# Normalising ahead of the gate, and dense jobs in nine slots, in a two-block transformer kernel on one core

## Chip, cores and metric

The kernel runs on one core of one Trainium2 chip. The metric is device time in microseconds (us); runs of one kernel are compared by their median.

## What is computed

The reference takes x of 512 tokens by 1024 through two blocks, all in fp32. What matters here is the attention of each layer and the dense projections around it.

```python
# first block: one layer, heads of 64, 8 pairs of (head, head) in the selected branch
o_a = nsa_attention(q_a, k_cmp, v_cmp, kv[2], kv[3], kv[4], kv[5], gates_a)
merged = gate_a * (o_a @ w_up_nsa) + gate_b * (o_b @ w_up_gla)
x = x + merged @ w_out
x = x + (silu(h @ w_ffn_gate) * (h @ w_ffn_up)) @ w_ffn_down
# second block: mla, swa, fox, mla; 16 heads each
s = einsum('bqhd,bkhd->bhqk', q_blk, k) * scale      # fox adds c_q - c_k, swa a slope and a window
p = softmax(where(k_pos <= q_pos, s, NEG_INF))
o = einsum('bhqk,bkhd->bqhd', p, v)
y = (o * silu(gate)) @ w_out                         # gate = x @ (its columns of w_in)
x = layernorm(ALPHA * x + y)
```

## The kernel before, in words

x, its transpose and all tiles of a layer live in SBUF. Every dense product is made of three fp32r matmuls (`mm3`, lines 385 to 388): a weight and an activation are each split in a high and a low part. A weight piece (up to 128 x 1024) is loaded by SyncE into one of three raw slots (`Wr`), cast by ScalarE to its high part (`Wh`, line 957), and its low part is made by GpSimd (`Wl`, line 1962, called a POOL piece in the prediction); five slots hold the results. ScalarE casts a piece when it comes to a wait: `weights` (949) casts all that are due by then, three pieces ahead of TensorE (`AHEAD`).

Attention goes by pairs of heads, p = 0 to 7. A pair takes these steps:
- score (517, or 880 in swa): TensorE makes the scores in PSUM; VectorE takes the maxima (1451); ScalarE makes the exps with their sums (1015; 1319 in swa).
- norm (`normalise`, 1458; in swa lines 1873 to 1879): VectorE inverts the sums and multiplies the probabilities P, eight instructions of 128 to 512 columns (line 1468); in swa four for each of two heads, called units (1879).
- turn (542): TensorE transposes P, 20 transposes (14 in swa), and ScalarE (1034, 1327) and VectorE (1438) copy them to PT.
- value (552, or 901 in swa): TensorE multiplies with V into a bank of its own. V in the prediction's formulas is the time at which these matmuls end.
- gate (`gate_values`, 1489, line 1492): VectorE multiplies that bank with the gate of the pair, GT. GT is made by the job g_p: 24 matmuls on TensorE, a tanh on ScalarE (1039), a product on VectorE (1487).
- out (`gated`, 1041 and 1494): the result is split in high and low (1013, 1435) for the output product w_out.
- prep (mla alone): two small products of this pair's queries and keys, 15 matmuls.

Jobs are dense products that fill TensorE while a pair's softmax goes through the other engines: g_p, q_p, k_p, v (in fox one job of 24 matmuls each, v of 96), `tail` and m0 to m7 in nsa. The order of all steps is written out before the program by `pair_steps` (101), once for each stage, and every engine walks the same list in order, doing its own part of each step. A turn waits for its pair's probabilities. PSUM has eight banks, which TensorE takes in a ring; a step waits until the reader of its bank is done. `before` runs what a step needs first (`need` pulls jobs from the front of the list, in its order, until the needed one has run), `fill` runs jobs up to a quota. There are five such stages: nsa (in the first block), mla0, swa, fox, mla1. What stands between the values of a pair and the turn of the next is the time in which exps and norm of the next pair are covered; it is called an interval below.

In fox the jobs are q0, k0, v0 (before the pairs) and then g0, q1, k1, g1, q2, k2, g2, q3, k3, v1, g3, q4, k4, g4, q5, k5, g5, q6, k6, g6, q7, k7, g7.

Of the kernel before, what the change touches and what calls it, by code (L numbers as in the profile page):

```python
# [97 lines left out]
                self.seen[sem.name] = value  # L98


def pair_steps(n, jobs, started, score, value, after=lambda p: [], gates=False, spread=7):

    left, steps, waiting = list(jobs[started:]), [], []
    total = len(left)

    def run():
        steps.append(("job", left.pop(0)))

    def before(these):
        for kind, x in these:
            if kind != "need":
                steps.append((kind, x))
            while kind == "need" and x in left:
                run()

    def fill(p):
        while left and (total - len(left)) * (spread + 1) < total * (p + 2):
            run()  # L120

    before(score(0))
    steps.append(("score", 0))
    steps.append(("norm", 0))
    before(after(0))
    fill(-1)
    for p in range(n):
        steps.append(("turn", p))
        if p + 1 < n:
            before(score(p + 1))  # L130
            steps.append(("score", p + 1))
        before(value(p))
        steps.append(("value", p))
        if gates:
            before([("need", f"g{p}")])
            steps.append(("gate", p))
            waiting.append(p)
        if p + 1 < n:
            steps.append(("norm", p + 1))
            before(after(p + 1))  # L140
        fill(p)
        for _ in range(8 if p == n - 1 else 2):
            if waiting and not left:
                steps.append(("out", waiting.pop(0)))
    return steps


def program(nc, A, out):
    top = ExitStack()
    with top:  # L150
# [139 lines left out]
        for dp in range(2):  # L290
# [12 lines left out]
            if dp == 0:  # L303
                gla_steps.append(("turned", dp))
        nsa_steps = pair_steps(8, ["tail"] + [f"m{f}" for f in range(8)], 0, lambda p: [], lambda p: [])
        mla_steps = pair_steps(
            8, ["g0", "g1", "g2", "v0", "g3", "v1", "g4", "g5", "g6", "g7"], 5,
            lambda p: [("prep", 0)] if p == 0 else [], lambda p: [("need", f"v{p // 4}")],
            lambda p: [("prep", p + 1)] if p < 7 else [], gates=True)
        swa_jobs = ["k0", "q0", "q1", "q2", "v", "q3", "g0", "g1", "k1", "q4", "g2", "q5", "g3", "q6", "g4", "q7", "g5", "g6", "g7"]  # L310
        swa_steps = pair_steps(8, swa_jobs, 4, lambda p: [("need", f"k{p // 4}"), ("need", f"q{p}")],
                               lambda p: [("need", "v")], gates=True)
        fox_jobs = ["q0", "k0", "v0", "g0"]
# [1738 lines left out]
```

## Time and profile before

| | us |
|---|---|
| median of 3 runs | 2010.88 (2010.56 to 2013.05) |
| profiled execution, its own time | 2010.83 |
| its span | 2009.0 |
| TensorE busy | 1870.5 (93%) |
| VectorE busy | 996.7 (50%) |
| ScalarE busy | 727.3 (36%) |
| GpSimd busy | 622.2 (31%) |
| mean granted TensorE clock, share of full speed | 0.966 |

The pairs of nsa lie between about 240 and 373 us of the span, those of mla0 between 975 and 1117, of swa between 1196 and 1353, of fox between 1450 and 1669, of mla1 between 1811 and 1952. The time around the span, 1.8 us, is start and end of the execution. Busy time of TensorE includes time at the lower clock.

### The profile page before, as it was taken

The page shows a single profiled execution, that of the slowest core. Times are in us where ns is not written, and L with a number is a line of the kernel's source. Part 1 is how long each engine was busy: PE and PEld are TensorE (multiplying, and loading weights), DVE is VectorE, ACT ScalarE, POOL GpSimd, SP SyncE. Part 2 cuts the span into 40 slices and gives each one's busy share as a digit, 9 for nine tenths or more (in the row PEclk, how much of TensorE's full clock was granted, in tenths as well). Part 3 has the DMA queues.
Part 4 walks back from the last instruction along what each step waited for, and adds up shares of the span by engine and source line. Part 5 has one row for each costly group of instructions (what it writes and reads, how often), then busy time and mean ns, then how long its engine had stood idle before and what let it go on. Part 6 is the DMA issues. An engine that isn't in the chain of part 4 may idle for free.

```text
span 2009.0 us, 24953 instructions
## 1 busy us (share of the span) xinstructions
PE 1870.5 (93%) x10060; PEld 1478.4 (74%) x10060; DVE 996.7 (50%) x1994; ACT 727.3 (36%) x1547; POOL 622.2 (31%) x296
## 2 busy tenths in 40 slices
PE   6998799999999999998999999989999999989997
PEld 5776666788888888877666787767777777866665
DVE  4457677322311101144767456675654444466675
ACT  4332354323322222253444234442342333334450
POOL 3331111244444453423212223223323223322221
PEclk9998799999999999999999999989999999999999
DMA  5321110243333332332212222112323222311111
GB/s 160 92 76 51 45 32 25 71 132 109 95 101 99 95 105 84 104 90 48 45 41 77 63 85 69 48 53 64 115 64 84 53 63 70 92 45 45 48 53 63
DMA packets 215027, 148.45 MB, mean 74 GB/s; under 512 B 51952, under 2 KB 197120, under 8 KB 214912
## 3 DMA queue, kind: packets, MB, share of 16 engines
q1 hardware_dynamic: 210160, 135.40, 24.1%
q10 hardware_dynamic: 4752, 11.46, 1.7%
q8 instruction: 79, 1.29, 0.3%
q14 instruction: 36, 0.29, 0.0%
HBM read 144.74 MB, written 2.10 MB: 73 GB/s over the span
## 4 chain that ended last, share of the span: by engine, by line
PE 72%; DVE 19%; ACT 6%; issue 1%; DMA 1%; POOL 0%; ACTq 0%; SPq 0%; DVEq 0%
PE PS L386 19%; PE PS L387 18%; PE PS L388 18%; PE PS L528 6%; PE PS L474 5%; DVE P L1468 3%; PE PS L557 2%; ACT P L1023 2%; DVE X L1401 1%; DVE P L1879 1%; PE PS L687 1%; DVE X L1405 1%; DVE ST L1428 1%; DVE X L1419 1%; DVE XTl L1413 1%
## 5 line engine op out<-in xcount | busy, mean ns | idle before, releaser
L1962 POOL TENSOR_TENSOR Wl<-Wr,Wh 128x1024 fp32r<-128x1024 f32 (+5 forms) x292 | 622.0, 2141 | 1349.4 <-ACT Wh L957 1349.2
L386 PE MATMUL PS<-XTl,Wh 128*128 128x512 f32 (+1 forms) x1096 | 416.9, 380 | 9.4 <-DVE XTl L1413 6.9
L387 PE MATMUL PS<-XTh,Wl 128*128 128x512 f32 (+1 forms) x1096 | 412.2, 376 | 0.0
L388 PE MATMUL PS<-XTh,Wh 128*128 128x512 f32 (+1 forms) x1096 | 411.6, 376 | 0.0
L957 ACT CAST Wh<-Wr 128x1024 fp32r<-128x1024 f32 (+5 forms) x292 | 267.7, 936 | 228.8 <-PE PS L388 207.3
L386 PEld LDWEIGHTS PS<-XTl,Wh 128*128 128x128 f32 x1096 | 209.8, 191 | 56.8 <-issue 12.9
L388 PEld LDWEIGHTS PS<-XTh,Wh 128*128 128x128 f32 x1096 | 209.8, 191 | 37.2
L387 PEld LDWEIGHTS PS<-XTh,Wl 128*128 128x128 f32 x1096 | 210.1, 192 | 35.2
L386 PE MATMUL PS<-Wl,XTh 128*128 128x512 f32 (+2 forms) x608 | 229.9, 378 | 5.0 <-DVE XTl L1413 5.0
L388 PE MATMUL PS<-Wh,XTh 128*128 128x512 f32 (+2 forms) x608 | 226.5, 372 | 0.0
L387 PE MATMUL PS<-Wh,XTl 128*128 128x512 f32 (+2 forms) x608 | 226.4, 372 | 0.0
L1023 ACT ACTIVATE P<-PS,sm 128x128 f32<-128x128 f32 (+3 forms) x256 | 131.5, 529 | 138.1 <-DVE sm L1455 138.0
L1468 DVE TENSOR_SCALAR P<-P,sm 128x128 f32<-128x128 f32 (+3 forms) x256 | 150.8, 660 | 1.1
L1455 DVE TENSOR_REDUCE sm<-PS 128x1 f32<-128x128 f32 (+3 forms) x256 | 107.3, 483 | 76.6 <-PE PS L532 76.5
L1419 DVE SCALAR_TENSOR_TENSOR X<-X,PS 128x512 f32<-128x512 f32 x64 | 43.4, 682 | 204.6 <-PE PS L388 204.2
L386 PEld LDWEIGHTS PS<-Wl,XTh 128*128 128x128 f32 x608 | 116.6, 192 | 26.9 <-DVE XTl L1413 6.5
L388 PEld LDWEIGHTS PS<-Wh,XTh 128*128 128x128 f32 x608 | 116.2, 191 | 17.9
L387 PEld LDWEIGHTS PS<-Wh,XTl 128*128 128x128 f32 x608 | 116.4, 191 | 16.8
L474 PE MATMUL PS<-CST,P 128*128 128x128 f32 x752 | 97.9, 289 | 31.7 <-DVE P L1879 17.1
L474 PEld LDWEIGHTS PS<-CST,P 128*128 128x128 f32 x752 | 90.0, 149 | 43.1 <-DVE P L1468 20.9
L1734 DVE TENSOR_TENSOR hf<-sg,PS 128x512 f32<-128x512 f32 x22 | 15.1, 688 | 188.2 <-PE PS L388 188.2
L1438 DVE COPY PT<-PS 128x512 f32<-128x512 f32 (+1 forms) x112 | 73.0, 669 | 49.2 <-PE PS L474 48.6
(311 smaller groups left out, 2481.0 us busy)
## 6 DMA issues: line engine op xcount, KB each, us to landing
Wr<-in_w_in SPq DMA_DIRECT2D x38, 512.0 KB, 3.7
Wr<-in_fox_w_in SPq DMA_DIRECT2D x32, 512.0 KB, 4.0
Wr<-in_w_ffn_gate SPq DMA_DIRECT2D x22, 512.0 KB, 3.8
Wr<-in_w_ffn_up SPq DMA_DIRECT2D x22, 512.0 KB, 3.8
Wr<-in_w_ffn_down SPq DMA_DIRECT2D x22, 512.0 KB, 3.5
Wr<-in_swa_w_in SPq DMA_DIRECT2D x20, 512.0 KB, 3.7
Wr<-in_mla_w_in SPq DMA_DIRECT2D x16, 512.0 KB, 4.0
Wr<-in_mla_w_out SPq DMA_DIRECT2D x16, 512.0 KB, 3.4
```

The source lines that it names most:

```text
L386: pe.matmul(o, l[0], r[1], start=start, stop=False)
L387: pe.matmul(o, l[1], r[0], start=False, stop=False)
L388: return pe.matmul(o, l[0], r[0], start=False, stop=stop)
L474: ins = pe.transpose(PS[b][0:m, c:c + p], src, IDN[0:p, 0:p])
L528: pe.matmul(b[:, c0:c0 + cols], *operands(u, i, cols), start=n == 0 and i != 1, stop=False)
L957: act.copy(Wh[i % W_SLOTS][:, 0:m], Wr[i % RAW_SLOTS][:, 0:m]).then_inc(*weight_hi.next(i))
L1023: act.activation(P[:, u, OFF[i]:OFF[i] + n], bank["score", s, p, u, max(i, 1)][:, c0:c0 + n], ACT.Exp, bias=sm[:, 4 * u + i:4 * u + i + 1] ...
L1419: ve.scalar_tensor_tensor(X[:, i, cs], X[:, i, cs], alpha, bank["y", s, i, c][:, :], mult, add).then_inc(*by_dve.next("y", s, i, c))
L1438: ve.tensor_copy(dst, src).then_inc(*by_dve.next(*key))
L1455: ve.reduce_max(sm[:, 4 * u + i:4 * u + i + 1], bank["score", s, p, u, max(i, 1)][:, c0:c0 + 128 * (i + 1)], AX.X, negate=True).then_inc(* ...
L1468: ve.tensor_scalar(q, q, sm[:, 16 + 4 * u + i:17 + 4 * u + i], None, mult).then_inc(*by_dve.next("probs", s, p))
L1962: raw.tensor_tensor(l[:, 0:m], r[:, 0:m], h[:, 0:m].bitcast(F), sub).then_inc(*weight_lo.next(i))
```

## The change

It is all in `pair_steps`. The list of steps is made in another order; no instruction is added or removed. norm of pair p + 1 now stands ahead of gate p. The quota of `fill` counts n + 1 = 9 slots in place of `spread` + 1 = 8, and in the last pair `fill` stands between turn and value. The out steps all come behind the last values (before, some stood in the last two intervals).

```diff
-def pair_steps(n, jobs, started, score, value, after=lambda p: [], gates=False, spread=7):
+def pair_steps(n, jobs, started, score, value, after=lambda p: [], gates=False):
...
     def fill(p):
-        while left and (total - len(left)) * (spread + 1) < total * (p + 2):
+        while left and (total - len(left)) * (n + 1) < total * (p + 2):
             run()
...
         before(value(p))
+        if p == n - 1:
+            fill(p)
         steps.append(("value", p))
+        if p + 1 < n:
+            steps.append(("norm", p + 1))
         if gates:
+            if p == n - 1:
+                steps.extend(("out", f) for f in range(p))
             before([("need", f"g{p}")])
             steps.append(("gate", p))
-            waiting.append(p)
         if p + 1 < n:
-            steps.append(("norm", p + 1))
             before(after(p + 1))
-        fill(p)
-        for _ in range(8 if p == n - 1 else 2):
-            if waiting and not left:
-                steps.append(("out", waiting.pop(0)))
+            fill(p)
+    if gates:
+        steps.append(("out", n - 1))
     return steps
```

The lists that result, each written from one turn to the next, at places that the prediction speaks of (job names stand for themselves):

```
fox,  before  turn 5 | k6 | score 6 | value 5 | gate 5 | norm 6 | g6 | q7
fox,  now     turn 5 | g5 | q6 | k6 | score 6 | value 5 | norm 6 | gate 5
swa,  before  turn 3 | score 4 | value 3 | g3 | gate 3 | norm 4 | q6
swa,  now     turn 3 | score 4 | value 3 | norm 4 | q5 | g3 | gate 3
swa,  before  turn 1 | score 2 | value 1 | gate 1 | norm 2 | k1 | q4
swa,  now     turn 1 | score 2 | value 1 | norm 2 | gate 1 | k1
mla,  before  turn 5 | score 6 | value 5 | gate 5 | norm 6 | prep 7 | g7 | out 0 | out 1
mla,  now     turn 5 | score 6 | value 5 | norm 6 | gate 5 | prep 7
mla,  before  turn 6 | score 7 | value 6 | gate 6 | norm 7 | out 2 | out 3
mla,  now     turn 6 | score 7 | value 6 | norm 7 | gate 6 | g7
nsa,  before  score 0 | norm 0 | tail | m0 | turn 0
nsa,  now     score 0 | norm 0 | tail | turn 0
nsa,  before  turn 7 | value 7
nsa,  now     turn 7 | m7 | value 7
```

Instruction order on VectorE in fox, between two turns late in the stage. Lines in the changed kernel are three higher. L1487 is the product of a job g, KT of a job k, L1492 the gate of a pair, L1468 the eight multiplications of norm. Before:

```order
L1438 COPY PT<-PS 128x2x256
L1438 COPY KT<-PS 128x512
L1455 TENSOR_REDUCE sm<-PS 128x1 x8
L1922 TENSOR_SCALAR MB<-CB,CST 96x512 x2
L1492 SCALAR_TENSOR_TENSOR GT<-GT,PS 128x512
L1460 RECIPROCAL sm<-sm 128x8
L1468 TENSOR_SCALAR P<-P,sm 128x128
L1468 TENSOR_SCALAR P<-P,sm 128x256
L1468 TENSOR_SCALAR P<-P,sm 128x128
L1468 TENSOR_SCALAR P<-P,sm 128x256
L1468 TENSOR_SCALAR P<-P,sm 128x384 x2
L1468 TENSOR_SCALAR P<-P,sm 128x512 x2
```

Now, from the PT copies to the last multiplications:

```order
L1441 COPY PT<-PS 128x2x256
L1490 SCALAR_TENSOR_TENSOR GT<-GT,PS 128x512
L1441 COPY KT<-PS 128x512
L1458 TENSOR_REDUCE sm<-PS 128x1 x8
L1925 TENSOR_SCALAR MB<-CB,CST 96x512 x2
L1463 RECIPROCAL sm<-sm 128x8
L1471 TENSOR_SCALAR P<-P,sm 128x128
L1471 TENSOR_SCALAR P<-P,sm 128x256
L1471 TENSOR_SCALAR P<-P,sm 128x128
L1471 TENSOR_SCALAR P<-P,sm 128x256
L1471 TENSOR_SCALAR P<-P,sm 128x384 x2
L1471 TENSOR_SCALAR P<-P,sm 128x512 x2
```

The product of job g has moved from behind the multiplications to ahead of the scores' maxima, with its job on TensorE; the gate now stands behind the multiplications.

ScalarE in mla0, from the exps of pair 6 to the turned copies of pair 6. CAST Wh is a weight piece, L1280 the queries of prep 7, L1039 the tanh of g7, L1013 the out steps, L1034 the turned copies. Before:

```order
L1023 ACTIVATE P,sm<-PS,sm 128x512 x2
L957 CAST Wh<-Wr 128x1024
L1280 ACTIVATE QT<-PS 128x512
L957 CAST Wh<-Wr 128x1024 x2
L1039 ACTIVATE GT<-PS 128x512
L1013 CAST XTh<-GT 128x512 x2
L1034 COPY PT<-PS 128x512 x2
```

Now:

```order
L1026 ACTIVATE P,sm<-PS,sm 128x512 x2
L960 CAST Wh<-Wr 128x1024
L1283 ACTIVATE QT<-PS 128x512
L960 CAST Wh<-Wr 128x1024
L1037 COPY PT<-PS 128x512 x2
```

One of three casts, the tanh and two out steps have left this interval; two casts of full width stay in it.

VectorE in swa, from the second unit's multiplications for pair 4 (L1879, now L1882) to the PT copies. Before, where the gate (L1487, L1492) stood ahead of both units:

```order
L1487 SCALAR_TENSOR_TENSOR GT<-GT,PS 128x512
L1492 SCALAR_TENSOR_TENSOR GT<-GT,PS 128x512
L1873 TENSOR_TENSOR sm<-sm 128x4
L1875 RECIPROCAL sm<-sm 128x4
L1879 TENSOR_SCALAR P<-P,sm 128x256 x4
L1873 TENSOR_TENSOR sm<-sm 128x4
L1875 RECIPROCAL sm<-sm 128x4
L1879 TENSOR_SCALAR P<-P,sm 128x256 x4
L1438 COPY PT<-PS 128x384 x2
```

Now:

```order
L1876 TENSOR_TENSOR sm<-sm 128x4
L1878 RECIPROCAL sm<-sm 128x4
L1882 TENSOR_SCALAR P<-P,sm 128x256 x4
L1876 TENSOR_TENSOR sm<-sm 128x4
L1878 RECIPROCAL sm<-sm 128x4
L1882 TENSOR_SCALAR P<-P,sm 128x256 x4
L1490 SCALAR_TENSOR_TENSOR GT<-GT,PS 128x512
L1495 SCALAR_TENSOR_TENSOR GT<-GT,PS 128x512
L1441 COPY PT<-PS 128x384 x2
```

The two gate products have moved from ahead of the normalisation to behind it, ahead of the PT copies.

## Rows read from the trace of the kernel before

**Rows 1.** The page, busy time, share of the span and instructions by engine.
```profile
PE 1870.5 (93%) x10060; PEld 1478.4 (74%) x10060; DVE 996.7 (50%) x1994; ACT 727.3 (36%) x1547; POOL 622.2 (31%) x296
```
**Rows 2.** Waits of TensorE: total us, times, longest; swa, mla0, mla1, fox, nsa, whole.
```profile
PE PS L474 <- DVE P L1879: 17.1, 6, 3.6
PE PS L901 <- DVE PT L1438: 0.7, 1, 0.7
...
PE PS L474 <- DVE P L1468: 4.9, 4, 3.5
...
PE PS L474 <- DVE P L1468: 5.0, 4, 3.5
...
PE PS L528 <- DVE KT L1438: 3.5, 4, 0.9
PE PS L557 <- DVE PT L1438: 0.9, 1, 0.9
...
PE PS L474 <- DVE P L1468: 4.7, 5, 1.0
...
PE PS L528 <- DVE KT L1438: 10.7, 6, 3.6
```
**Rows 3.** Timeline of mla0's last interval: start us, length us, instruction, [idle before, releaser].
```profile
1107.03 2.46 DVE L1468 TENSOR_SCALAR P<-P,sm 128x128 f32<-128x128 f32 x8
...
1109.54 0.69 PE L474 MATMUL PS<-CST,P 128*128 128x128 f32 x2 [3.51 <-DVE P L1468]
```
**Rows 4.** Timeline of fox's last interval: multiplications, POOL piece, job's first matmul, turn 7.
```profile
1658.30 4.60 DVE L1468 TENSOR_SCALAR P<-P,sm 128x128 f32<-128x128 f32 x8
...
1659.04 2.51 POOL L1962 TENSOR_TENSOR Wl<-Wr,Wh 128x1024 fp32r<-128x1024 f32 x1 [11.19 <-ACT Wh L957]
...
1657.23 0.50 PE L386 MATMUL PS<-XTl,Wh 128*128 128x512 f32 x1
...
1662.95 0.33 PE L474 MATMUL PS<-CST,P 128*128 128x128 f32 x1
```
**Rows 5.** Windows: length, busy by engine, then granted PE clock, DMA share, GB/s.
```profile
1234.80:1354.80 120.00, 105.49 (x659) 86.53 (x659) 85.44 (x181) 55.52 (x152) 26.54 (x11) 0.91 0.16 50
1235.00:1243.00 8.00, 7.96 (x64) 6.81 (x65) 5.29 (x12) 1.89 (x5) 0.00 (x0) 0.79 0.03 10
1346.80:1354.80 8.00, 7.26 (x47) 6.27 (x47) 4.29 (x8) 4.55 (x9) 0.00 (x0) 0.57 0.20 66
1109.50:1117.50 8.00, 7.96 (x38) 5.70 (x39) 3.59 (x6) 2.73 (x5) 0.00 (x0) 0.62 0.00 0
1945.60:1953.60 8.00, 8.00 (x45) 6.17 (x46) 5.10 (x9) 3.91 (x7) 0.00 (x0) 0.82 0.01 2
975.00:983.00 8.00, 7.99 (x37) 3.51 (x37) 1.15 (x4) 1.72 (x8) 0.00 (x0) 0.57 0.08 19
```
**Rows 6.** Timeline of swa before turn 2: values 1, second unit's multiplications, copies of job k1.
```profile
1240.02 1.75 PE L901 MATMUL PS<-PT,V 128*64 128x128 f32 x28
...
1247.76 3.29 DVE L1879 TENSOR_SCALAR P<-P,sm 128x256 f32<-128x256 f32 x4
1250.97 2.84 DVE L1438 COPY KT<-PS 64x512 f32<-64x512 f32 x4
```
**Rows 7.** Timeline: cast before mla0's turn 2; multiplications with three and two POOL pieces.
```profile
1023.76 1.04 ACT L957 CAST Wh<-Wr 128x1024 fp32r<-128x1024 f32 x1
...
1087.23 8.89 DVE L1468 TENSOR_SCALAR P<-P,sm 128x128 f32<-128x128 f32 x8
...
1457.57 6.75 DVE L1468 TENSOR_SCALAR P<-P,sm 128x128 f32<-128x128 f32 x8
```
**Rows 8.** Timeline of nsa: first multiplications, turn 0, turn 2.
```profile
252.99 4.60 DVE L1468 TENSOR_SCALAR P<-P,sm 128x128 f32<-128x128 f32 x8
...
257.77 0.49 PE L474 MATMUL PS<-CST,P 128*128 128x128 f32 x3
...
289.52 0.66 PE L474 MATMUL PS<-CST,P 128*128 128x128 f32 x4 [0.78 <-DVE P L1468]
```

More of the change, by code:

```diff
@@ L98, in wait_ge @@
                 self.seen[sem.name] = value
-def pair_steps(n, jobs, started, score, value, after=lambda p: [], gates=False, spread=7):
-    left, steps, waiting = list(jobs[started:]), [], []
+def pair_steps(n, jobs, started, score, value, after=lambda p: [], gates=False):
+    left, steps = list(jobs[started:]), []
     total = len(left)
```

## Prediction

> **What bounds the kernel now.** The page's busy line comes first: TensorE is busy for 1870.5 of 2009.0 us [rows 1]. A change that adds and removes no instruction can therefore move only two things: time in which TensorE stands idle, and time in which it runs at the lower of its two clocks (1.2 instead of 2.4 GHz). So I read the waits of TensorE by stretch [rows 2]. In the pairs of swa it waits 17.1 us for the normalised probabilities and 0.7 us for a copy; in the pairs of the two mla stages 4.9 and 5.0 us; in fox 3.5 us for the keys' copy and 0.9 us for a PT copy, but never for the probabilities; in nsa 4.7 us for the probabilities. Those waits are what the change shuffles, so each stage is one term.
>
> **What a pair needs as cover.** Call V the time at which a pair's values matmuls end. The next turn needs the next pair's eight multiplications of `normalise`. In mla's last interval, where no dense job stands after the values, turn 7 waits 3.51 us for them; they take 2.46 us [rows 3]. In fox's last interval the same eight take 4.60 us, because a POOL subtraction (a weight's low part, 2.51 us) starts 0.74 us after them; still nothing waits, because one dense job of 24 matmuls stands there, from 1657.23 to 1662.95, 5.7 us [rows 4]. So: without a job the wait is 3.5 us without a POOL piece and 5.6 us with one; one job hides both.
>
> **What a wait costs beside itself.** Each of the five waits of 3.5 to 3.6 us that I looked at (swa's turns 1 and 7, mla0's and mla1's turn 7, and the keys' wait before mla0's first scores [rows 2]) is followed by eight us at a granted clock of 0.79, 0.57, 0.62, 0.82 and 0.57 [rows 5]. One minus the clock, times 8 us, gives 1.7, 3.4, 3.0, 1.4 and 3.4 us lost: mean 2.6. I take 2.7, as the mla1 wait before the first scores is like mla0's, and as bounds 1.4 and 3.4. That price goes on every wait of about 3.5 us or more, and nothing on one of 1 us or less. Over all pairs of swa from 1234.8 to 1354.8 the clock was 0.91, so 10.8 us, of which some 0.8 fell into idle time: 10.0 us lost [rows 5].
>
> **fox: 4 x (3.5 + 2.7) = +24.8 us.** This is the largest term, and it isn't what the diff seems to be about. The quota falls from p + 2 eighths of the 21 jobs to p + 2 ninths, while `before(score(p + 1))` still forces q and k of the next pair, and the g queued ahead of them. From p = 3 on that forcing alone exceeds the quota, so `fill(p)` runs nothing: g, q and k stand between turn and scores, and between values and the next turn nothing is left but norm and gate. Before, g and q (48 matmuls, 11.2 us) stood there, and one job at p = 6. That makes turns 4, 5, 6 and 7 waits like mla's 3.51 us. No POOL piece lengthens them: ScalarE's order has no cast between these exps and the turned copies, it casts before the exps, during k's job. Bounds: 4 x (3.5 + 1.4) = 19.6 and 4 x (3.5 + 3.4) = 27.6. The keys' copy now stands bare before five score steps instead of four, +0.9 us; the 0.9 us before the last values goes, since g7 stands there and no out step is ahead of the PT copies on VectorE. These two cancel.
>
> **swa: -12.0 us.** Before, 17.1 + 0.7 of waits and 10.0 of clock, 27.8. The reason for the waits at turns 1 and 3 to 6 is that `need g{p}` puts job g_p between values and norm, so VectorE's gate (behind TensorE's job and ScalarE's tanh) stands ahead of the normalisation. Now norm goes first and 48 matmuls (11.2 us) cover it; at turn 2 of before, the values ended at 1241.8 and the second unit's multiplications, with a POOL piece in their way, at 1251.05, 9.3 us after V [rows 6]. So those five waits go. Two stay or come: turn 7 has one job ahead as before (3.6 us, the longest of swa's six [rows 2]), and turn 2 now has k1 alone instead of k1 and q4, the same case: 2 x 3.6 = 7.2. At turn 2 gate 1 (0.7 us), four KT copies (2.84) [rows 6] and two PT copies (0.6 each) now begin only when norm ends, 4.7 us in all, while turn and scores take 3.5: values 2 waits 1.2 us. At turns 3 to 6 the second score bank is the one that the gate reads, and the gate now runs last, behind tanh and the g product: it ends 2.2 us after the jobs (a tanh of 0.6, two products of 0.7, their starts), the scores begin 1.75 us after them: 4 x 0.45 = 1.8. Then 0.3 us before w_out, since all out steps now come after the last values. Clock for two waits: 5.4. Sum 15.9, so 15.9 - 27.8 = -11.9, taken as -12.0; bounds -14.6 and -10.6 by the clock.
>
> **mla, twice: +0.3 us together.** Turn 7 gets g7 ahead of it, so 3.5 us and its clock loss (3.0 and 1.4 us) go. But g6 and g7 have left other intervals. Turn 4 now has prep 5 alone, like turn 2 before, 0.3 us, and turn 5 loses its 0.3. The dear one is turn 6, with prep 7 alone: 15 matmuls, 3.7 us from V. There the pieces to cast are full ones, 1024 wide: one as the exps end, and one behind prep 7's product (at turn 2 such a cast began at 1023.76, just too late to hurt [rows 7]). Two subtractions on POOL stretch the eight multiplications: with three of them they took 8.89 us, with two in fox 6.75 [rows 7]. From V + 1.0 us, with 6.7, they end at V + 7.7: a wait of 4.0 us where 0.8 (the rest of the 4.9) stood behind 39 matmuls. Before: 4.9 + 3.0 + 5.0 + 1.4 = 14.3. After: 2 x (0.3 + 0.3 + 4.0 + 2.7) = 14.6. Here a rule can be weighed against the trace. In the trace eight multiplications cost 2.46 us alone and 4.60, 6.75 and 8.89 with one, two and three pieces: about 2.1 more for each. The Trainium skill (SBUF — State Buffer, Who interferes with whom) says that VectorE and GpSimd share one port pair as an exclusive lock and that the later one blocks fully; by it alone the two pieces would cost their whole 4.8 us and the wait would be 4.5 us, the total 1.0 us more. The sum keeps the measured 6.7.
>
> **nsa: +6.9 us.** m0 no longer stands before turn 0, m7 stands between turn 7 and the last values. Before, m0 ran while turn 0 waited for probabilities that took 4.60 us from 252.99 because m0's cast fed a POOL piece [rows 8]. That cast goes with m0, so they end at 255.5 and turn 0 starts 2.3 us earlier than its 257.8. m7 costs a whole job at the end, +5.7: the 0.8 us wait there is for CT, whose transposes come after m7, and stays. Turn 6's interval now casts a full piece where a half one stood: +0.8, the wait of turn 2 [rows 8]. And TensorE, which m0 kept busy at the lower clock, idles 7 us and starts turn 0 low: +2.7. -2.3 + 5.7 + 0.8 + 2.7 = 6.9.
>
> **Moving gate behind norm in mla and fox:** zero. VectorE's reciprocal follows ScalarE's last exp there, and the gate fitted ahead of it; behind it, it meets 0.2 to 1.2 us of VectorE idle before the maxima. If that slack were gone, 0.7 us per pair of mla and fox would be the price. Weight loads on SP and POOL keep their order and count; 24 to 72 matmuls per cluster are met by three raw slots now as before, priced at zero.
>
> **Sum:** 24.8 - 12.0 + 0.3 + 6.9 = +20.0 us. The profiled execution took 2010.83 us for its span of 2009.0, the median is 2010.88, so both give **2031 us**. A measurement of this kernel can tell about 0.2%, 4 us, from no change.
>
> **Rivals.**
> *The clock doesn't fall (faster).* Nine waits carry the 2.7 us: four in fox, two in swa, two in mla, one in nsa. If the drops of before have another cause and the new waits bring none, the sum is 20.0 - 9 x 2.7 = -4.3, so 2006.6 us. The sign turns at 0.5 us per wait. Against it: all five waits of 3.5 to 3.6 us were followed by a drop [rows 5]. Chance 0.06.
> *VectorE gets through between two POOL pieces at mla's turn 6.* If the second cast comes later, the multiplications take 4.6, the wait is 1.9 and the clock may hold: 2 x (2.1 + 2.7) = 9.6 less, 2021.4 us. For it: at turn 2 the second piece came just too late. Against: there the first one was only 256 wide. Chance 0.15.
> *A POOL piece does reach fox's bare normalisations*, by a late weight load that delays the cast: 4 x 2.1 = 8.4 more, 2039 us. Chance 0.07.
> *The nine slots aren't made.* In fox they aren't, by the order itself; that is in the forecast. In the other three stages they are.
>
> **How the numbers follow.** The forecast has 0.72. The clock's bounds alone, 9 x (1.4 - 2.7) and 9 x (3.4 - 2.7), reach from 2019 to 2037; the second rival lies inside, and the range takes in most of the third: 2019 to 2038. Faster by over 0.2%: 0.07 (the first rival, and a little for several terms at their lower ends), within: 0.04, slower: 0.89.
>
> **What would show it.** Right: in fox four TensorE waits of 3.4 to 3.7 us for P, none in swa but two of about 3.6, one of about 4 before turn 6 in each mla and none before turn 7, and granted clocks under 0.85 behind each. Wrong: fox's turns 4 to 7 start right behind values, or the clock stays at 1.00 behind them; then the total falls to before's level.

## The result and the profile after

| | before | change |
|---|---|---|
| median | 2011.97 us (4 runs) | 2024.35 us (4 runs, 2022.71 to 2024.8) |
| ratio, with its 95% interval | | 1.0052 (1.0039 to 1.0064) |
| profiled execution, its span | 2010.83, 2009.0 | 2024.30, 2022.5 |
| mean granted clock | 0.966 | 0.964 |

By the two medians the change costs 12.4 us. The ratio, which takes in more than these medians, says some 10 us; the four runs of the kernel before lie between 2010.6 and 2015.7 us. It was forecast slower, by 20 us, in a range from 2019 to 2038 us. So the sign and the range held, and the step was forecast too large by some 7 us. The page's busy line and then the waits of TensorE in the pairs of swa, mla0, mla1, fox and nsa, in the order of [rows 2]:

```profile
PE 1871.7 (93%) x10060; PEld 1480.7 (73%) x10060; DVE 984.6 (49%) x1994; ACT 726.3 (36%) x1547; POOL 621.8 (31%) x296
```

```profile
PE PS L477 <- DVE P L1882: 7.0, 2, 3.6
PE PS L883 <- DVE GT L1495: 1.0, 4, 0.3
PE PS L389 <- DVE XTl L1438: 0.4, 1, 0.4
...
PE PS L477 <- DVE P L1471: 4.7, 3, 4.0
...
PE PS L477 <- DVE P L1471: 4.7, 3, 4.0
...
PE PS L477 <- DVE P L1471: 14.1, 4, 3.5
PE PS L531 <- DVE KT L1441: 4.4, 5, 0.9
...
PE PS L477 <- DVE P L1471: 12.9, 7, 7.2
```

swa's waits for probabilities fell from 17.1 to 7.0 us; fox, which never waited for them, waits four times for 14.1 us. Granted clocks in the eight us behind each long wait (columns as in [rows 5]): swa's turns 2 and 7, fox's turns 4 to 7, turn 6 of mla0 and of mla1, nsa's turn 0:

```profile
1253.90:1261.90 8.00, 8.00 (x64) 6.73 (x65) 7.74 (x16) 1.93 (x5) 0.00 (x0) 0.79 0.22 66
1337.00:1345.00 8.00, 8.00 (x37) 7.10 (x38) 2.19 (x4) 2.12 (x3) 2.40 (x1) 0.82 0.25 75
1575.90:1583.90 8.00, 8.00 (x40) 7.22 (x41) 2.58 (x4) 2.12 (x3) 2.39 (x1) 0.82 0.01 2
1607.10:1615.10 8.00, 7.97 (x33) 7.31 (x34) 2.64 (x4) 2.11 (x3) 2.39 (x1) 0.63 0.01 2
1639.70:1647.70 8.00, 7.96 (x38) 7.26 (x39) 2.66 (x4) 2.12 (x3) 2.39 (x1) 0.79 0.00 0
1671.30:1679.30 8.00, 8.00 (x39) 7.27 (x40) 2.57 (x4) 2.12 (x3) 2.40 (x1) 0.81 0.00 0
1102.90:1110.90 8.00, 8.00 (x48) 6.24 (x48) 4.32 (x9) 1.81 (x5) 0.00 (x0) 0.70 0.18 66
1943.30:1951.30 8.00, 8.00 (x52) 5.89 (x56) 4.27 (x9) 2.47 (x9) 0.00 (x0) 0.79 0.17 61
257.40:265.40 8.00, 8.00 (x48) 6.00 (x50) 6.08 (x16) 2.03 (x7) 0.00 (x0) 0.76 0.00 0
```

Behind every one of them the clock was below 1.00. With 8 us times one minus the clock, the nine cost 1.7, 1.4, 1.4, 3.0, 1.7, 1.5, 2.4, 1.7 and 1.9 us: 16.7 us, 1.9 each. Before nsa's turn 0 the clock was at its lower level (0.50) already all through the wait, so that wait did not bring it down.

The stages, each from its first score matmul to its last values matmul (in nsa the last of L560, L557 before), worked out from the TensorE records. The numbers in brackets are the terms of the forecast.

| stage, us | before | change | difference |
|---|---|---|---|
| nsa | 133.07 | 139.67 | +6.6 (+6.9) |
| mla0 and mla1 | 142.12, 140.66 | 142.45, 140.76 | +0.4 (+0.3) |
| swa | 156.79 | 142.56 | -14.2 (-12.0) |
| fox | 218.72 | 239.99 | +21.3 (+24.8) |
| all else | 1217.7 | 1217.1 | -0.6 (0) |
| span | 2009.0 | 2022.5 | +13.5 (+20.0) |

### The profile page after: what moved, and what is told of

Its sections match the earlier page's. It is cut to its first block, busy times and chain, and to the rows that moved or that the text cites. A ratio compares the mean times of both kernels' runs of the same rounds, so it can differ in the third digit from the quotient of the medians.

```text
span 2022.5 us, 24946 instructions
## 1 busy us (share of the span) xinstructions
PE 1871.7 (93%) x10060; PEld 1480.7 (73%) x10060; DVE 984.6 (49%) x1994; ACT 726.3 (36%) x1547; POOL 621.8 (31%) x296
## 4 chain that ended last, share of the span: by engine, by line
PE 74%; DVE 17%; ACT 6%; issue 2%; DMA 1%; POOL 0%; ACTq 0%; SPq 0%; DVEq 0%
PE PS L389 20%; PE PS L391 19%; PE PS L390 19%; PE PS L531 6%; PE PS L477 5%; DVE P L1471 3%; ACT P L1026 3%; PE PS L560 2%; PE PS L690 1%; DVE X L1404 1%; DVE X L1408 1%; DVE ST L1431 1%; DVE X L1422 1%; DVE XTl L1416 1%; PE PS L535 1%
## 5 line engine op out<-in xcount | busy, mean ns | idle before, releaser
L477 PE MATMUL PS<-CST,P 128*128 128x128 f32 x752 | 104.4, 301 | 43.3 <-DVE P L1471 36.3
L1471 DVE TENSOR_SCALAR P<-P,sm 128x128 f32<-128x128 f32 (+3 forms) x256 | 142.1, 627 | 1.1
L477 PEld LDWEIGHTS PS<-CST,P 128*128 128x128 f32 x752 | 96.4, 157 | 54.9 <-DVE P L1471 44.8
L390 PEld LDWEIGHTS PS<-Wh,XTl 128*128 128x128 f32 x608 | 115.2, 189 | 16.7
```

Of the source, the lines that this page charges most:

```text
L390: pe.matmul(o, l[1], r[0], start=False, stop=False)
L477: ins = pe.transpose(PS[b][0:m, c:c + p], src, IDN[0:p, 0:p])
L1471: ve.tensor_scalar(q, q, sm[:, 16 + 4 * u + i:17 + 4 * u + i], None, mult).then_inc(*by_dve.next("probs", s, p))
```

## The experiments

Stage lengths are counted as above, in the profiled execution. Times are medians of 4 or 10 runs (one in experiment 10) with the ratio to the kernel before and its 95% interval. The first two take the change's two halves apart.

**1. norm ahead of gate, alone.** In the kernel before, one step is moved.

```diff
         steps.append(("value", p))
+        if p + 1 < n:
+            steps.append(("norm", p + 1))
         if gates:
...
-            steps.append(("norm", p + 1))
```

> The kernel before with one edit: norm of the next pair ahead of the gate; jobs and out steps stand where they stood. Theory (each stage is its own term, the wait for P is what counts): swa loses the waits at turns 1 and 3 to 6 (13.5 us) and their clock, keeps 3.6 at turn 7, so 17 to 20 us less from first score to last values; nsa, mla and fox change by under 0.5 us each; total 1992 to 1996 against 2011. Rival (the gain of the change in swa comes from the nine slots, not from the order): swa changes by under 5 us and the total stays above 2006.

Measured: 1992.04 us, 0.9898 (0.9883 to 0.9912). swa takes 135.12 us, 21.7 less than before; nsa, mla0, fox and mla1 stay within 0.9 us (132.91, 142.05, 218.75, 141.53). Waits of TensorE in swa:

```profile
PE PS L475 <- DVE P L1880: 3.6, 1, 3.6
PE PS L902 <- DVE PT L1439: 0.7, 1, 0.7
```

What follows: this half is a gain of 20 us, all of it in swa, where the gate was what VectorE did first. It is a little more than the 17 to 20 us expected there. One wait stays, at turn 7. mla1 grew by 0.9 us, more than the 0.5 expected; below it turns out that an mla stage differs by as much from one execution to the next.

**2. nine slots, alone.** The change, with norm put back behind gate.

```diff
-        if p + 1 < n:
-            steps.append(("norm", p + 1))
...
         if p + 1 < n:
+            steps.append(("norm", p + 1))
             before(after(p + 1))
```

> The changed kernel with norm put back behind the gate: nine slots and late out steps alone. Theory: nsa +6.6, mla +0.3 each and fox +21 as in the change; in swa norms now stand behind jobs g of 24 matmuls that are last of their interval, so turns 3 to 6 wait some 5 to 7 us each with their clock: swa 15 to 30 us longer than in the kernel before, total 2055 to 2075. Rival (the norm order is what costs fox its time): fox falls back to its length of before, and the total is below 2030.

Measured: 2060.09 us, 1.024 (1.0223 to 1.0257). fox 240.18 and nsa 139.27 us, as in the change; swa 179.96, 23.2 more than before. Waits of TensorE in swa:

```profile
PE PS L476 <- DVE P L1881: 33.2, 7, 5.9
```

What follows: the nine slots cost 32 us with norm ahead of gate (1992.04 to 2024.35) and 48 without it. The loss in fox and nsa belongs to them alone. In swa the two halves do not add up: norm ahead of gate is worth 21.7 us with eight slots and 37.4 with nine (179.96 to 142.56).

**3. fox's jobs by eighths.** `pair_steps` gets a parameter; the four other stages stay as in the change.

```diff
-        while left and (total - len(left)) * (n + 1) < total * (p + 2):
+        while left and (total - len(left)) * slots < total * (p + 2):
...
-                               lambda p: [("need", f"v{p // 4}")], gates=True)
+                               lambda p: [("need", f"v{p // 4}")], gates=True, slots=8)
```

> The changed kernel, but fox fills by eighths as before, so g and q stand again between values and the next turn. Theory: the four waits of 3.5 us for P go, with their clock loss of 7.6 us; fox is 21 to 23 us shorter than in the change, a little under its length of before (0.9 us of the PT wait before the last values gone); total 2002 to 2004. Rival (the late out steps or the gate behind norm cost in fox): fox stays more than 4 us longer than before.

Measured: 2001.20 us (0.8 under the range expected), 0.9944 (0.9929 to 0.9959); fox 217.74 us, 22.3 less than in the change. TensorE's waits in fox hold none for P:

```profile
PE PS L531 <- DVE KT L1441: 3.5, 4, 0.9
```

What follows: fox's loss is the quota; neither the later out steps nor the gate behind norm cost anything there. With it taken back the kernel is faster than before, so one stage turns a gain of 11 us into a loss of 12.

**4. nsa's jobs by eighths.** The same parameter, given to nsa alone.

```diff
-        nsa_steps = pair_steps(8, ["tail"] + [f"m{f}" for f in range(8)], 0, lambda p: [], lambda p: [])
+        nsa_steps = pair_steps(8, ["tail"] + [f"m{f}" for f in range(8)], 0, lambda p: [], lambda p: [], slots=8)
```

> The changed kernel, but nsa fills by eighths as before: m0 stands before turn 0 again, nothing between turn 7 and the last values. Theory: the 7.2 us wait at turn 0 and its clock go, nsa is 6 to 7 us shorter than in the change (133 us), total 2017 to 2019. Rival (m7 at the end costs what m0 at the start did, so that nsa's length doesn't hang on it): nsa within 2 us of the change's 139.7.

Measured: 2016.81 us, 1.0012 (1.0002 to 1.0021); nsa 133.02 us against 139.67. So nsa's whole loss comes from the places of its jobs: every m stands one interval earlier again, m0 before turn 0 and none behind turn 7.

**5. TensorE kept at work in fox's waits.** Ahead of turns 4 to 7, 14 matmuls whose result nothing reads.

```diff
                 elif kind == "turn":
+                    if x >= 4:
+                        b = take(("busy", x))
+                        e.wait_ge(*free(b))
+                        for _ in range(14):
+                            pe.matmul(PS[b][:, :], XT[0][:, 0, 0:128], XT[0][:, 0, :], start=True, stop=True)
+                        give(b)
                     turn(s, x, P)
```

> The changed kernel with 14 idle-time matmuls (128x512, into a PSUM bank that nobody reads) ahead of each of fox's turns 4 to 7, some 3.2 us each, so that TensorE is busy while it would wait 3.5 us. Theory (beside the wait itself the lower clock costs 7.6 us in fox): the clock stays at 1.00 behind these turns, the turns start at the same distance from the values, and fox is 6 to 8 us shorter than in the change, total 2016 to 2018. Rival (the clock's fall has another cause, or costs nothing): fox within 2 us of the change's length.

Measured: 2016.74 us, 1.0019 (1.0009 to 1.0028); fox 232.59 us, 7.4 less than in the change. The turns start no earlier behind their values, since the multiplications take as long as they did. What is gone is the clock loss behind them, here at turn 4:

```profile
1575.20:1583.20 8.00, 8.00 (x46) 6.97 (x47) 2.59 (x4) 2.21 (x4) 2.40 (x1) 1.00 0.06 13
```

What follows: of fox's 21.3 us, 7.4 are the clock, against 7.6 read off the change's windows and 10.8 in the forecast; the rest is 14.1 of waiting (the shorter PT wait and the keys' copies make up for each other). It is idle TensorE that lets the clock fall, not the turn's small matmuls.

**6. A later cast in mla.** ScalarE's turned copies of pair 6 wait for TensorE without first casting what is due, so the second weight piece is cast behind them.

```diff
-                    after(turned_full, s, p, g)
+                    if s[:3] == "mla" and p == 6:
+                        e.wait_ge(turned_full.at(s, p, g))
+                    else:
+                        after(turned_full, s, p, g)
```

> The changed kernel, but in both mla stages ScalarE waits for turn 6 without casting the weight piece that is due, so that piece is cast during the exps of pair 7 and only one POOL piece meets the multiplications before turn 6. Theory (each POOL piece adds about 2.1 us to the eight multiplications): they take 4.6 instead of 6.7 us, the wait before turn 6 is 1.9 to 2.0 instead of 4.05 us, each mla 2.1 us shorter, or up to 4 if the clock then holds; total 2016 to 2020. Rival (the wait of 4 us comes from something else, such as prep 7's copy or a bank): wait and length unchanged.

Measured: 2016.23 us, 1.0014 (1.0004 to 1.0023); mla0 and mla1 137.11 us each, 5.3 and 3.7 less than in the change; the 5.3 is more than the 4 that the theory allowed. mla0 before turn 6, first in the change, then here:

```profile
1096.11 6.68 DVE L1471 TENSOR_SCALAR P<-P,sm 128x128 f32<-128x128 f32 x8
...
1096.85 4.93 POOL L1965 TENSOR_TENSOR Wl<-Wr,Wh 128x1024 fp32r<-128x1024 f32 x2 [13.90 <-ACT Wh L960]
...
1102.85 0.90 PE L477 MATMUL PS<-CST,P 128*128 128x128 f32 x3 [4.05 <-DVE P L1471]
```

```profile
1095.11 4.59 DVE L1474 TENSOR_SCALAR P<-P,sm 128x128 f32<-128x128 f32 x8
...
1095.86 2.51 POOL L1968 TENSOR_TENSOR Wl<-Wr,Wh 128x1024 fp32r<-128x1024 f32 x1 [13.91 <-ACT Wh L960]
...
1099.76 2.40 PE L477 MATMUL PS<-CST,P 128*128 128x128 f32 x20 [1.96 <-DVE P L1474]
```

With one POOL piece the wait is 2.0 us instead of 4.05, and behind it the clock stays up, in mla0, where it was 0.70, and in mla1; the third row is behind fox's turn 4 in the same execution:

```profile
1099.80:1107.80 8.00, 8.00 (x64) 4.90 (x66) 4.77 (x11) 3.87 (x12) 2.34 (x1) 1.00 0.27 104
1936.20:1944.20 8.00, 8.00 (x64) 4.90 (x66) 4.77 (x11) 3.84 (x11) 2.34 (x1) 1.00 0.27 105
...
1572.20:1580.20 8.00, 7.96 (x46) 6.96 (x47) 2.65 (x4) 2.17 (x4) 2.39 (x1) 1.00 0.09 13
```

So the second piece costs 2.1 us by VectorE, and the clock that its longer wait brings down 2.4 and 1.7 us: 4.5 of the 5.3, and 3.8 for the 3.7. The missing 0.8 us lies elsewhere. Behind the 3.6 us wait before mla0's first scores, which the change doesn't touch, the clock was lower in the profiled execution of the change than in those of the kernel before and of this experiment (in this order, ten us each):

```profile
982.94:992.94 10.00, 10.00 (x44) 4.85 (x45) 1.96 (x6) 1.93 (x9) 0.00 (x0) 0.56 0.07 16
...
975.01:985.01 10.00, 10.00 (x48) 5.20 (x49) 2.90 (x8) 2.88 (x13) 0.00 (x0) 0.66 0.07 15
...
982.87:992.87 10.00, 10.00 (x48) 5.31 (x49) 2.91 (x8) 2.88 (x13) 0.00 (x0) 0.66 0.07 16
```

That is 1.0 us (4.4 against 3.4) and belongs to the execution. Experiments 3, 4, 5 and 10 leave the change's mla as it is, and there mla0 took 141.48, 140.78, 140.79 and 140.79 us, mla1 140.79, 140.81, 140.78 and 142.14. Against six of these eight the later cast gains 3.7 us.

fox holds a surprise (the row behind its turn 4, above): a wait of 3.52 us, of the very same kind as in the change, and no loss. fox took 238.52 us there, 1.5 less than in the change. swa's turn 2 has the same: a wait of 3.58 us, and 1.00 behind it. What that did to swa is told below, with the forecast's swa term.

**7. Jobs placed by cover.** The change's order of steps, with the count of jobs that have run by each interval written out for mla and swa: where the cover would be bare stands a job. nsa and fox go by eighths.

```diff
-        while left and (total - len(left)) * (n + 1) < total * (p + 2):
+        while left and total - len(left) < (plan[p + 1] if plan else total * (p + 2) / n):
...
-            lambda p: [("prep", p + 1)] if p < 7 else [], gates=True)
+            lambda p: [("prep", p + 1)] if p < 7 else [], gates=True, plan=(1, 2, 2, 2, 2, 3, 4, 5, 5))
...
-                               lambda p: [("need", "v")], gates=True)
+                               lambda p: [("need", "v")], gates=True, plan=(1, 3, 5, 7, 9, 11, 13, 15, 15))
```

> The changed order of norm, gate and out steps, with jobs placed by what an interval has to cover and not by a quota: nsa and fox by eighths as before; swa with v alone before turn 0 and then two jobs in each interval; mla with none in the intervals before turns 2 to 4, and g5, g6, g7 before turns 5, 6 and 7. Theory (waits for P and their clock add up by stage): swa without a wait for P, 131 to 134 us instead of 156.8; mla with three waits of 0.3 us, some 135 us each instead of 142 and 141; fox 217.8, nsa 133; total 1970 to 1976. Rival (VectorE or ScalarE is near its own limit in swa or mla once TensorE doesn't wait): new waits for PT copies or scores take back half, total above 1980.

Measured: 1979.01 us, 0.9832 (0.9811 to 0.9854). swa 134.62, mla0 and mla1 137.95 and 137.97, fox 217.78, nsa 132.95 us. Waits for the probabilities over the whole execution:

```profile
PE PS L477 <- DVE P L1471: 11.8, 14, 1.1
```

What follows: no such wait is longer than 1.1 us any more, and swa has none. The total is 3 us above the range that was expected, and mla is where: 138 instead of 135 us in each stage. Its waits for P are 1.06, 1.06, 0.30 and 0.81 us in mla0, 3.2 in all where three of 0.3 were expected, so 2.3 of the 3 us are waits of TensorE. The 3.4 us that the clock costs behind the wait of 3.6 us before the first scores were there before as well; the next run takes them away.

**8 and 9. Idle work in other waits.** On top of run 7, matmuls that nothing reads: 14 ahead of each mla stage's first scores (8), and 28 more ahead of each mla stage's query products (9).

```diff
                     elif kind == "score":
+                        if x == 0:
+                            b = take((s, "busy"))
+                            e.wait_ge(*free(b))
+                            for _ in range(14):
+                                pe.matmul(PS[b][:, :], XT[0][:, 0, 0:128], XT[0][:, 0, :], start=True, stop=True)
+                            give(b)
```

> The kernel with jobs placed by cover, and ahead of each mla stage's first scores 14 more matmuls of 128x512, whose result nothing reads, in the 3.6 us in which TensorE waits for the keys' copy. In that kernel's trace the eight us behind this wait ran at a granted clock of 0.57, twice. Theory (an idle TensorE is what lets the clock fall): the 8 us behind it run at 1.00, 2 x 8 x 0.43 = 6.9 us saved, so about 1972 us against 1979, and each mla stage itself, counted from its first scores, gets 3.4 shorter: 134.5. Rival (the low clock there belongs to the narrow matmuls of the first scores): no change, 1979 us and 137.95.

> As the run with idle work before the mla scores, and 28 such matmuls more in the wait of 7.2 us ahead of each mla stage's query products. Behind that wait the clock was 0.82 and 0.78 for 8 us. Theory: 1.4 and 1.8 us saved, so 3 us under the run before, about 1969 us. Rival: the same time as that run.

Measured: 1972.95 us, 0.9796 (0.9779 to 0.9814), and 1969.99 us, 0.9789 (0.9773 to 0.9806). In both, mla0 and mla1 take 134.76 to 134.78 us, 3.2 less than in run 7. Behind the 3.6 us, where the clock was 0.57 [rows 5], in run 8:

```profile
980.10:988.10 8.00, 8.00 (x53) 4.92 (x54) 3.37 (x8) 4.05 (x15) 0.00 (x0) 1.00 0.09 20
1782.20:1790.20 8.00, 8.00 (x53) 4.91 (x54) 3.37 (x8) 4.04 (x15) 0.00 (x0) 1.00 0.10 23
```

What follows: the clock as a price of idle time holds outside fox as well, at two places that the change doesn't touch. The gain of run 9 over run 8, 3.0 us, is as expected, but their intervals overlap, so the medians alone don't show it. The windows do: behind the wait of 7.2 us the clock was 0.75 in both mla stages of run 8, and 1.00 in both of run 9:

```profile
944.90:952.90 8.00, 7.37 (x32) 5.99 (x33) 0.62 (x3) 1.74 (x3) 2.40 (x1) 1.00 0.00 0
1746.70:1754.70 8.00, 7.30 (x31) 5.92 (x32) 0.62 (x3) 1.67 (x3) 2.39 (x1) 1.00 0.00 1
```

**10. fox's waits filled in part.** As experiment 5, with 3, 6, 9 and 4 matmuls ahead of turns 4, 5, 6 and 7.

```diff
-                        for _ in range(14):
+                        for _ in range({4: 3, 5: 6, 6: 9, 7: 4}[x]):
```

> The change, and ahead of fox's turns 4, 5, 6 and 7 three, six, nine and four matmuls whose result nothing reads, so that of each wait of 3.5 us some 2.8, 2.0, 1.3 and 2.5 us stay idle. In the change the clock behind the four waits cost 1.4, 3.0, 1.7 and 1.5 us. Theory (a short idle stretch costs no clock: behind waits of 1.96 and 2.4 us it stayed at 1.00): turns 5, 6 and 7 keep 1.00, turn 4 may not, fox takes 232.6 to 234 us against 240.0 in the change. Rival (the loss goes with the idle time in proportion): 4.4 us of the 7.6 stay, fox 236.8 us.

Measured, one run: 2019.64 us; fox 235.69 us. TensorE was idle for 2.62, 1.93, 1.24 and 2.39 us before the four turns, and behind them:

```profile
1574.50:1582.50 8.00, 7.97 (x39) 7.22 (x40) 2.65 (x4) 2.13 (x3) 2.39 (x1) 0.81 0.01 2
1605.80:1613.80 8.00, 7.98 (x46) 6.95 (x47) 2.64 (x4) 2.17 (x4) 2.40 (x1) 1.00 0.08 10
1635.70:1643.70 8.00, 8.00 (x46) 7.00 (x47) 2.59 (x4) 2.24 (x4) 2.39 (x1) 1.00 0.11 28
1665.50:1673.50 8.00, 8.00 (x38) 7.22 (x39) 2.62 (x4) 2.12 (x3) 2.41 (x1) 0.79 0.00 0
```

What follows: neither theory. Turns 5 and 6 kept 1.00 as the first said, turn 7 didn't. The loss doesn't shrink with the idle time, it is there whole (1.5 and 1.7 us) or not at all. The 2.39 us of turn 7 did bring it, where 2.4 us elsewhere had not. 232.59 us of experiment 5 and these two losses make 235.8, as measured.

## Why the prediction was right, and where its sizes were off

**fox, +24.8 forecast, +21.3 measured.** The mechanism is the one forecast: turns 4 to 7 and no others wait, 3.51 or 3.52 us each, behind multiplications of 2.46 us with no POOL piece in them.

```profile
1573.35 2.46 DVE L1471 TENSOR_SCALAR P<-P,sm 128x128 f32<-128x128 f32 x8
...
1575.86 0.90 PE L477 MATMUL PS<-CST,P 128*128 128x128 f32 x3 [3.51 <-DVE P L1471]
```

So 4 x 3.5 was exact. The keys' copy took 0.9 us more and the PT wait went, as said. The term that was mis-sized is the clock: 4 x 2.7 = 10.8, measured 7.6 by the windows and 7.4 by experiment 5. The bound of 1.4 was near two of the four.

**swa, -12.0 forecast, -14.2 measured.** The waits for P are there, at turns 2 and 7, 3.59 and 3.41 us. Before, turn and scores of a pair took 3.34 us from the first transpose to the first values matmul, at clock 1.00 and without a wait. In the change turn 2 took 5.02 us (first two rows), and turns 3 to 6 took 4.07 each, of which the next two rows are turn 4's scores; the last row is the same scores in experiment 1, where nothing holds them up:

```profile
1253.87 2.64 PE L477 MATMUL PS<-CST,P 128*128 128x128 f32 x14 [3.59 <-DVE P L1882]
1256.44 2.52 PE L883 MATMUL PS<-KT,QT 64*128 64x128 f32 x16
...
1289.99 0.49 PE L883 MATMUL PS<-KT,QT 64*128 64x128 f32 x2
1290.73 1.78 PE L883 MATMUL PS<-KT,QT 64*128 64x128 f32 x14 [0.26 <-DVE GT L1495]
...
1284.24 1.79 PE L881 MATMUL PS<-KT,QT 64*128 64x128 f32 x16
```

The bank that the gate reads holds back the third score matmul, which starts 0.74 us after the first. The values begin 2.45 us after the first score here and 1.72 in experiment 1, so the pair loses 0.73 us. The view of waits calls only 0.26 of it idle, since the matmul before the wait counts as running. So the bank wait cost 4 x 0.73 = 2.9 us, not the 1.0 of the view and not the 1.8 forecast: this term was too small.

The step "values 2 waits 1.2 us" can be read off experiment 6, where the clock stayed at 1.00 behind turn 2's wait:

```profile
1251.12 1.75 PE L477 MATMUL PS<-CST,P 128*128 128x128 f32 x14 [3.58 <-DVE P L1885]
1252.79 1.35 PE L883 MATMUL PS<-KT,QT 64*128 64x128 f32 x10
1254.48 1.13 PE L883 MATMUL PS<-KT,QT 64*128 64x256 f32 x6 [0.33 <-DVE KT L1444]
...
1251.10:1259.10 8.00, 7.63 (x66) 6.11 (x67) 7.74 (x16) 1.87 (x5) 0.00 (x0) 1.00 0.23 66
```

The values began 4.50 us after the turn, 1.2 more than 3.34, because VectorE was at its copies. So the 1.2 us was right in size, though TensorE loses it in the scores. In the change the same stretch took 1.7 us more than 3.34: the lower clock added 0.5 us there and not another 1.7, because the slow turn and scores filled what would have been waiting. The forecast had added the two, 1.2 + 2.7 = 3.9. Turn 7's clock cost 1.4 us (2.7 forecast), and the 0.3 us before w_out lies outside the stage.

Before, the stage lost as much as forecast: experiment 1's 135.12 us less its waits of 3.6 and 0.7 and some 1.6 of clock is 129.2 us without any loss, so the kernel before lost 27.6 (27.8 forecast) and the change loses 13.4 (15.9 forecast): 7.0 of waits for P, 1.7 at turn 2, 2.9 for the bank, 1.4 of clock, and 0.4 that stays open.

**mla, +0.3 forecast, +0.4 measured.** Turn 6 waits 4.05 us in both stages, turn 7 not at all. Eight multiplications with two POOL pieces took 6.68 us, as taken (6.7). What a piece does shows in a single multiplication of 384 columns. The first row is the one that meets the piece in experiment 6's mla0, the second the two of fox's turn 4 in the change, which meet none (0.7 us together, 410 ns each):

```profile
1096.04 2.54 DVE L1474 TENSOR_SCALAR P<-P,sm 128x384 f32<-128x384 f32 x1
...
L1471 DVE TENSOR_SCALAR P<-P,sm 128x384 f32<-128x384 f32 x2 | 0.7, 410 | 0.0
```

The blocked multiplication starts 0.2 us after the piece (1095.86, 2.51 us long) and ends at 1098.58, 0.2 us after the piece's end; the multiplications around it take their usual time. The Trainium skill (SBUF — State Buffer, Who interferes with whom) says that the later of the two fully blocks, and the trace agrees. What was wrong is the price that the prediction made of it, 4.8 us for two pieces and a wait of 4.5: the blocked multiplication takes 2.54 instead of 0.41 us, so a piece costs 2.1 and not its whole length. The sum had the measured price.

The clock losses were 2.4 and 1.7 us, 2.7 taken. That the term came out so closely is luck. An mla stage with the same steps took from 140.8 to 142.5 us in the change and experiments 3, 4, 5 and 10, and the two of the kernel before took 140.7 and 142.1, so +0.4 us for both can't be told from nothing. In mla0 the waits fell by 0.2 us and the clock's loss at the long wait by 0.6 (3.0 to 2.4), and 1.0 us more was lost behind the keys' wait before the first scores (0.56 against 0.66, experiment 6). The second rival, VectorE passing between two pieces, did not happen; experiment 6 made it happen: 2.1 us of wait less, and the clock held. For both stages it came to 9.0 us (9.6 forecast), or some 7.4 against the more usual 140.8 us.

**nsa, +6.9 forecast, +6.6 measured.** From the first scores to turn 0 it is 16.7 us and was 18.8, so 2.2 less (-2.3 forecast); the turn now starts behind 7.19 us of idle. Turn 6 waits 1.1 us (0.8 forecast), m7 adds its 5.7, the clock 1.9 (2.7 forecast): 6.5 us, 6.6 measured.

**Gate behind norm, 0 in mla and fox.** Experiment 1 bears it out for fox: with only that moved, it is at 218.75 us against 218.72. mla0 is 0.1 us shorter and mla1 0.9 longer, both inside what executions differ by.

**The sum.** Of the 6.5 us between +20.0 and +13.5, fox is 3.5 (3.2 of it the clock), swa 2.2 and nsa 0.3, and mla takes back 0.1; 0.6 lies outside the stages. The first scores of nsa, ahead of which no experiment changes anything, start between 238.7 and 242.7 us in the kept traces, so 0.6 us there means nothing. The forecast's single price of 2.7 us for a wait's clock, the mean of five, was the weak step: the nine new ones average 1.9. The first rival (no clock loss) is out: behind all nine the clock was low, and experiment 5 gives 7.4 us back. The third (a POOL piece in fox) did not happen.

## What to carry to other kernels

A step list for in-order engines is best planned by cover, interval by interval: write down what the slowest chain needs (here 3.5 us, or 5.6 with one GpSimd piece beside it) and what independent work stands there, and don't spread jobs by an even quota, which leaves some intervals bare as soon as dependences pull the jobs elsewhere. Put the work that someone waits for ahead of the work that nobody does: this half of the change is worth 20 us alone, and with jobs placed by cover the kernel is at 0.983 of before. Cost a long wait of TensorE with the clock behind it, but don't add the clock to a wait that the slow stretch itself fills. Where the wait can't be avoided, matmuls that nothing reads, where they fit inside it, bring that part back (0.979 at the end).

## What was not expected of the hardware

- Equal waits don't have equal consequences. Behind 3.5 us before fox's turns the next 8 us ran at 0.82, 0.63, 0.79 and 0.81, and once, in experiment 6, at 1.00; swa's turn 2, 3.6 us, had 0.79, and in experiment 6 1.00. Behind 2.39 us (experiment 10) it was 0.79; behind 2.40 us ahead of a projection of fox (run 7) the row reads 1.00:

```profile
1390.40:1398.40 8.00, 8.00 (x66) 8.00 (x67) 2.02 (x4) 3.41 (x6) 2.48 (x2) 1.00 0.48 131
```

- The kernel before shows the same in swa: behind its waits of 2.65, 2.35, 2.27 and 2.65 us at turns 3 to 6 the next 8 us ran at 0.79, 0.79, 1.00 and 0.81. The prediction had looked only at the waits of 3.5 us and more.
- The length of the single wait doesn't decide alone. Waits of 1.24, 1.93 and 1.96 us in fox and mla had no loss behind them, but in nsa, where TensorE had been busy for only 5.3 of the 8 us before, a wait of 1.74 us (run 7) was followed by this:

```profile
249.30:257.30 8.00, 6.68 (x22) 5.27 (x23) 6.23 (x19) 6.50 (x20) 0.00 (x0) 0.57 0.00 0
```

- What decides in each case isn't settled by these runs.
- A shorter wait doesn't bring a smaller loss: where filling left 2.62 us of fox's 3.51 us idle, the clock behind it was as low as in the change (0.81 and 0.82).
